# A hybrid transformer layer pair on one core: three gated tile pairs of the input projection moved behind the queries and between the attention's first steps, and gated scaling and memory scaling moved from GpSimd to VectorE and ScalarE

## What is computed

```python
h = rmsnorm(x, norm_mix_g)
proj = h @ w_in                                   # 1024 -> 1988 columns
q, k, v, qi, ki, wi, glu = jnp.split(proj, cuts, axis=-1)
q, k, qi, ki = partial_rope(...)                  # 8 query heads of 64, one key head
a_out = dsa_attention(q, k, v, qi, ki, wi)        # an indexer of 4 heads picks the keys, then softmax
ga, gg = jnp.split(glu, 2, axis=-1)               # 512 + 512 columns
u = causal_dwconv(ga * jax.nn.sigmoid(gg), conv_b_w, conv_b_b)   # 31 taps, 512 channels
b_out = jax.nn.silu(layernorm(u, ln_b_g, ln_b_b))
x = x + jnp.concatenate([a_out, b_out], axis=-1) @ w_out
m = rmsnorm(mem, norm_mem_g)                      # 256 tokens; kc = m @ w_k_cross, vc = m @ w_v_cross
```

## Time and profile before

| | us |
|---|---|
| median of 3 runs | 1429.32 (1425.02 to 1429.35) |
| the profiled execution's own time | 1433.47 |
| its span in the profile | 1431.7 |
| mean granted clock of TensorE | 0.982 of 2.4 GHz |
| busy in the span: TensorE / VectorE / GpSimd / ScalarE | 1369.7 / 789.3 / 606.7 / 539.3 |

### The profile page before, as it was taken

How to read it: one execution, slowest core, us unless ns; L and a number is a source line. 1 busy time by engine, 2 the same in 40 slices (tenths; PEclk the granted TensorE clock), 3 DMA queues, 4 the chain that set the end, 5 groups by cost and what they waited for, 6 DMA issues and landing times.

```text
span 1431.7 us, 18120 instructions
## 1 busy us (share of the span) xinstructions
PE 1369.7 (96%) x6240; PEld 1100.0 (77%) x6240; DVE 789.3 (55%) x1083; ACT 539.3 (38%) x843; POOL 606.7 (42%) x295
## 2 busy tenths in 40 slices
PE   7998888999999999999999999999999999999997
PEld 5787766877678888888888777677778888888885
DVE  6698984253366777777534488555463333333232
ACT  4445667243343232333223353434343223233221
POOL 3587981232144444444444333111234444444341
PEclk9999998999999999999999999999999999999998
DMA  6122320221122232223332222111122322233221
GB/s 218 45 89 88 104 81 23 74 74 66 38 88 89 88 103 91 100 101 106 102 101 82 82 74 75 44 45 45 45 76 100 101 89 103 89 107 101 102 88 73
DMA packets 31874, 121.18 MB, mean 85 GB/s; under 512 B 3536, under 2 KB 3664, under 8 KB 31568
## 3 DMA queue, kind: packets, MB, share of 16 engines
q1 hardware_dynamic: 31392, 119.55, 24.6%
q10 hardware_dynamic: 432, 0.96, 0.3%
HBM read 118.40 MB, written 2.10 MB: 84 GB/s over the span
## 4 chain that ended last, share of the span: by engine, by line
PE 70%; issue 14%; POOL 7%; DVE 5%; ACT 3%; DMA 1%; POOLq 0%; SPq 0%; DVEq 0%; ACTq 0%
PE acc L1627 58%; POOL weights_low L588 4%; PE acc L1775 3%; POOL conv L637 2%; PE aux L1997 1%; PE aux L2017 1%; DVE aux L1160 1%; DVE left L1491 1%; PE aux L1861 1%; PE aux L1999 1%; DMA weights_raw<-w 1%; PE aux L1831 1%; PE aux L1681 0%; PE aux L2033 0%; PE aux L2007 0%
## 5 line engine op out<-in xcount | busy, mean ns | idle before, releaser
L588 POOL TENSOR_TENSOR weights_low<-weights_raw,weights_high 128x1024 fp32r<-128x1024 f32 (+1 forms) x204 | 524.9, 2573 | 794.2 <-ACT weights_high L665 791.2
L665 ACT CAST weights_high<-weights_raw 128x1024 fp32r<-128x1024 f32 (+1 forms) x202 | 222.0, 1099 | 523.3 <-PE acc L1627 502.5
L1627 PE MATMUL acc<-a_high,weights_high 128*128 128x512 f32 x976 | 391.1, 401 | 5.5 <-POOL weights_low L588 3.0
L1627 PE MATMUL acc<-a_high,weights_low 128*128 128x512 f32 x976 | 382.2, 392 | 0.0
L1627 PE MATMUL acc<-a_low,weights_high 128*128 128x512 f32 x976 | 381.8, 391 | 0.0
L1627 PEld LDWEIGHTS acc<-a_high,weights_high 128*128 128x128 f32 x976 | 184.6, 189 | 47.8 <-issue 6.2
L1627 PEld LDWEIGHTS acc<-a_low,weights_high 128*128 128x128 f32 x976 | 184.7, 189 | 39.8 <-issue 2.6
L1627 PEld LDWEIGHTS acc<-a_high,weights_low 128*128 128x128 f32 x976 | 184.3, 189 | 39.2
L1133 DVE TENSOR_TENSOR residual<-acc,residual 128x512 f32<-128x512 f32 (+1 forms) x56 | 38.5, 688 | 183.0 <-PE acc L1627 146.3
L1627 PE MATMUL acc<-h_high,weights_high 128*128 128x512 f32 x352 | 137.6, 391 | 0.0
L1627 PE MATMUL acc<-h_high,weights_low 128*128 128x512 f32 x352 | 137.0, 389 | 0.0
(11 more groups left out here) (346 smaller groups left out, 1898.5 us busy)
## 6 DMA issues: line engine op xcount, KB each, us to landing
weights_raw<-w SPq DMA_DIRECT2D x172, 512.0 KB, 3.2
weights_raw<-w SPq DMA_DIRECT2D x32, 704.0 KB, 4.1
residual<-xT SPq DMA_DIRECT2D x8, 256.0 KB, 7.0
out<-y_tok SPq DMA_DIRECT2D x4, 512.0 KB, 3.6
mem_raw<-memT SPq DMA_DIRECT2D x1, 1024.0 KB, 5.5
mem_tok<-mem SPq DMA_DIRECT2D x1, 1024.0 KB, 7.5
lru_weights<-blockdiag ACTq DMA_DIRECT2D x1, 512.0 KB, 3.4
sine<-positions ACTq DMA_DIRECT2D x1, 256.0 KB, 7.0
```

The costliest lines, as they stand in the source:

```text
L588: g.tensor_tensor(weights_low[:, s, 0:cols], weights_raw[:, s, 0:cols], weights_high[:, s, 0:cols].bitcast(F32), ALU.subtract).then_inc(we ...
L665: a.copy(weights_high[:, s, 0:cols], weights_raw[:, s, 0:cols]).then_inc(weight_high, 1)
L1627: last = t_.matmul(acc[:, bank, 0:cols], w[:, s, wide], x_[:, k0 + k, 0:cols], start=start and k == opens and n == 0, stop=stop and k == c ...
```

## The change

It has four parts.

1. **Chunks and list.** Chunks are ordered `kiwi`, `qiT`, `qiT`, `kv`, the first gated pair (4, 5), the four queries (6 to 9), the other three gated pairs (10 to 15). Tiles 5 and 6 are cut into pieces between the `index` items. The attention's steps begin after tile 9 and the first half of tile 10; eleven half tiles of the gated pairs and the 32 half fills stand between the steps. Twelve of the 16 `best` rounds move into steps 0 to 7, the taps into steps 8 to 27, `mean` from step 25 to 27, and the rest of the layer norm and the out-projection with it by two steps.
2. **Scaling.** VectorE evicts the gated tiles and multiplies by `row_factor` at once (`glu_out`). Memory is scaled in ScalarE's cast, and VectorE makes its low part. GpSimd's items for both are gone.
3. **Head.** TensorE finishes tile 0 before tile 1. ScalarE's squares stand behind all high parts, between which it casts chunks 2 and 3 and copies tiles 0 and 1. `add_x` is interleaved with the angle reduction. The positions are loaded by SyncE's queue behind x. `spread` (the sines) stands behind tile 3.
4. **Convolution.** VectorE has 79 taps (blocks 1, 2 and 17 taps of 3), ScalarE with GpSimd 45.

```diff
-        SHARED_TAPS = 9
-        PRODUCTS = [(1, k) for k in range(SHARED_TAPS)] + [(0, k) for k in range(TAPS)]
-        CONV = [(n, k) for n in (2, 3) for k in range(TAPS)] + [(1, k) for k in range(SHARED_TAPS, TAPS)]
+        SHARED_TAPS = 14
+        PRODUCTS = ([(0, k) for k in range(20)] + [(3, k) for k in range(SHARED_TAPS)]
+                    + [(0, k) for k in range(20, TAPS)])
+        CONV = [(n, k) for n in (1, 2) for k in range(TAPS)] + [(3, k) for k in range(SHARED_TAPS, TAPS)]
...
+        FIRST_PLAN = [("tile", 0, 0, KB), ("tile", 1, 0, KB), ("mem_root",), ("tile", 2, 0, KB),
+                      ("key_turn", 0), ("query_turn", 0), ("tile", 3, 0, 4), ("sum",), ("mem_high", 0, 4),
+                      ("tile", 3, 4, KB), ("mem_low", 0, 4), ("spread",), ("key", 0), ("query", 0),
+                      ("tile", 4, 0, 4), ("query_turn", 1), ("mem_high", 4, 8), ("wi",), ("query", 1),
+                      ("tile", 4, 4, KB)]
...
+        FIRST_PLAN += [("causal",), ("tile", 6, 6, KB), ("gate", 0), ("glu", 0), ("key_turn", 1), ("best",),
+                       ("tile", 7, 0, 4), ("key", 1), ("mem_low", 4, 8), ("query_turn", 2), ("query", 2), ("v",),
+                       ("tile", 7, 4, KB), ("best",), ("tile", 8, 0, 4), ("query_turn", 3), ("query", 3),
+                       ("best",), ("tile", 8, 4, KB), ("mem_spread",), ("tile", 9, 0, 4), ("query_turn", 4),
+                       ("query", 4), ("best",), ("tile", 9, 4, KB)]
+        FILLS = [("tile", n, 4 * half, 4 * half + 4) for n in range(10, 16) for half in range(2)]
+        FILLS += [("fill", n, 4 * half, 4 * half + 4) for n in range(2 * KB) for half in range(2)]
...
-        FILLS_AT = (1, 1, 2, 1, 2, 1, 2, 1, 1, 1, 2, 1, 1, 1, 2, 1, 1, 1, 1, 0, 1, 1, 1, 0, 1, 0, 1, 0, 1, 0, 1, 0)
+        FILLS_AT = (1, 2, 2, 2, 2, 2, 2, 2, 1, 2, 1, 1, 1, 2, 1, 1, 1, 1, 1, 2, 1, 1, 1, 1, 1, 1, 1, 1, 2, 1, 1, 1)
+        BEST_AT = (2, 1, 2, 1, 2, 1, 2, 1)
+        FIRST_TAP, LAST_TAP, FIRST_PRODUCT, LAST_PRODUCT = 8, 27, 0, 25
...
+            if step in (2, 4, 7):
+                FIRST_PLAN += [("gate", (step + 1) // 2 - (step == 7)), ("glu", (step + 1) // 2 - (step == 7))]
...
+            square_x(0)
+            square_x(1)
+            high_next(0, 0)
+            square_x(2)
+            square_x(3)
+            a.copy(kiwi[:], acc[:, 0]).then_inc(tile_out[0], 1)
+            square_x(4)
+            high_next(0, 1)
+            a.copy(qiT[:, 0], acc[:, 1]).then_inc(tile_out[1], 1)
...
-                        act.wait_ge(mem_scaled, k + 1)
-                        a.copy(m_high[:, k], mem_raw[:, k]).then_inc(mem_high, 1)
+                        act.wait_ge(memT_in, 16)
+                        a.activation(m_high[:, k], mem_raw[:, k], ACT.Copy, scale=col("g_mem", k)
+                                     ).then_inc(mem_high, 1)
...
+                        v.scalar_tensor_tensor(m_low[:, k], mem_raw[:, k], col("g_mem", k),
+                                               m_high[:, k].bitcast(F32), ALU.mult, ALU.subtract
+                                               ).then_inc(mem_low, 1)
+                elif what == "glu_out":
+                    b, s = j // 2, j % 2
+                    dve.wait_ge(chunk_done, GLU[j] + 1)
+                    v.tensor_tensor(gate[:, b] if s else glu[:, b, TAPS - 1:TAPS - 1 + T], acc[:, s],
+                                    row_factor[:], ALU.mult).then_inc(tile_out[s], 1)
...
+                for k in range(2, KB):
+                    part(0, k, 0)
+                    part(1, k, 0)
+                    part(0, k, 2)
+                    part(0, k - 2, 1)
+                part(0, KB - 2, 1)
+                part(0, KB - 1, 1).then_inc(chunk_done, 1)
                 for k in range(KB):
+                    part(1, k, 1)
+                for k in range(KB):
+                    last = part(1, k, 2)
+                last.then_inc(chunk_done, 1)
```

192 lines of the change are left out of this document (84 added, 108 removed).

## The result

| | median us | lowest to highest | runs |
|---|---|---|---|
| before, beside it | 1428.95 | 1425.02 to 1430.89 | 7 |
| after | 1437.47 | 1433.17 to 1442.6 | 7 |

The ratio is 1.006, 95% interval 1.0045 to 1.0075: the change costs 8.5 us, and I had forecast 1.3. The profiled execution of after took 1433.41 us, as long as that of before (1433.47), so the two traces have to be compared place by place and not at their ends.

The account below looks back on a forecast made before the run. TensorE, busy 96% of the span, leaves only idle and slow stretches to win; VectorE is fullest after 130 us. Head +7.4, VectorE's run -3.0, tail -2.6 give +1.8; 1429.3 plus that less 0.5 is 1430.6 us, range 1419 to 1437.

Parts of the forecast that it names:

- Head: Start to the last index score's causal mask: sines behind tile 3 delay VectorE, so the end comes 7.4 us later.
- the index wait: TensorE before the first index product: a new wait of about 4.2 us for VectorE, with a slow clock behind it.
- VectorE's run: Causal mask to the mean's start: 143.5 us of work plus 10 idle, 153.5 instead of 156.5, a gain of 3.0 us.
- Tail: Mean to out-projection: more half fills in the last steps leave less work behind the wait, a gain of 2.6 us.
- The same 9 us chain: Tail, from the factor's spread to the end of TensorE's wait: unchanged at 9 us, from +20.3 to +29.3 after the mean.
- the stall itself: Tail, TensorE's wait for ScalarE behind the spread: claimed to stay near 5 us.
- The stall at 192.75: TensorE's 2.74 us stall, where vc's copy now has wider steps beside it: should shrink, 0.5 us gained.
- GpSimd's relief at nothing: Attention: taking gated and memory scalings off GpSimd was valued at zero, since VectorE's listed waits had no GpSimd in them.
- B: Rival: VectorE idles 4 us instead of 10 and the tail's half-clock stretch doesn't come; 1421.7 us, chance 0.33.
- C: Rival, steps 0 to 7: gated tiles wait for VectorE's evictions, engines in lockstep, +6.3 us; 1436.9 us, chance 0.17.
- D: Rival, steps 0 to 7: ScalarE's three pairs of table loads aren't hidden, 7.7 us; 1438.3 us, chance 0.07.
- the wait behind the spread: Sign in the tail that the forecast is right: TensorE waits 5 us for ScalarE behind the factor's spread.

Follow-up runs that it names:

- e12: The changed kernel with sines early, memory's work later, sines times the factors in PSUM, and three fills moved to steps 11, 14 and 21; 1426.74 us.
- e14: e12 with four pieces of one tile between the index scores instead of six of two, tile 6 whole behind the causal mask; 1428.32 us.
- e18: e14 with one selection round of VectorE moved from step 0 to in front of the second key's rope; 1428.89 us.
- e17: e13 with three taps moved from VectorE to products of ScalarE and GpSimd (12 shared taps instead of 9); 1420.29 us.
- e6: The changed kernel with gated tiles again copied by ScalarE and scaled on GpSimd, all else as changed; 1437.81 us.
- e16: e12 with three taps moved from VectorE to products of ScalarE and GpSimd (17 shared taps instead of 14); 1431.15 us.
- e13: e9 with the eight gated tiles evicted and scaled by VectorE instead of ScalarE's copy and GpSimd's scaling; 1420.41 us.
- e15: e12 with the three moved fills put back, five again in steps 28 to 31; 1431.44 us.
- e5: The changed kernel with both sines right behind the root of the sums and memory's work behind the first keys and queries; 1437.33 us.
- e9: e8 with VectorE multiplying the sines by the rows' factors in PSUM and copying the factors to SBUF afterwards; 1419.60 us.
- e1: The changed kernel with the sines moved to right behind the norm's root; 1441.55 us.
- e3: The kernel before with the change's new head alone, the sines right behind the norm's root; 1423.45 us.
- e8: e3 with GpSimd's eight memory scalings in pairs behind every third index score; 1424.31 us.

## Why the prediction was wrong

- **Head, +7.4 forecast, +5.4 measured.** Right in kind. Tile 2 began at 20.6 (23.6 forecast), the sine product at 39.9 (42.4), the index wait was 4.18 us (4.2) with the half-clock pieces behind it, the mask at 66.9 (68.9). The 2 us come from tiles 0 and 1, which ended 3 us sooner than I had reckoned. What I had not seen is that this shift isn't all lost time: 3.3 us of it are tile 6's pieces done ahead (e12 against e14).
- **VectorE's run, -3.0 forecast, -1.5 measured** (155.0 us for 156.5). Its work was 143.5 us to the tenth; its idle time 11.5 instead of 10. TensorE had 44.2 us of work in steps 0 to 7, not 40.3, as much as VectorE there. The mean at 221.9 lies in the forecast 221 to 223. The sum was near, but not the picture of one bound engine: a shorter or earlier list of VectorE gained at most 0.7 us at the mean (e18), nothing in e17, and the mean came later where GpSimd got the work (e6, e16); adding work to it in the old order cost nothing (e13).
- **Tail, -2.6 forecast, +4.5 measured** (34.4 us became 38.9). This is the step that failed, by 7.1 us, as much as the whole error of 7.2 (8.5 for 1.3); the errors of head and run, -2.0 and +1.5, nearly cancel, which is luck. "The same 9 us chain ends at +29.3": the chain was neither the same nor in time. It starts where the factor's spread ends (TensorE, before and then after):

```profile
236.38 1.11 PE L1681 MATMUL aux<-ident,small 128*128 128x128 f32 x8
```

```profile
244.38 1.11 PE L1695 MATMUL aux<-ident,small 128*128 128x128 f32 x8
```

  Counted from the mean that is +19.5 and +23.6, where I had +20.3 for after: the sum for the mean took 5.40 us instead of 3.70, a half fill more (1.5 us) stands ahead of the variance, and the next one, behind the variance, ran mostly at half clock (0.63 us a piece). From there to the end of the wait it took 11.15 us and not 9: "the stall itself stays, near 5 us" left out that the last fill's cast and two evictions, 2.1 us, now stand on ScalarE between the silus and the copy TensorE waits for; it waited 7.18 us. Behind the wait came 4.2 us and not 3.0, again at half clock. These are 3.3, 2.1 and 1.2 us, and before's own tail was 0.5 shorter than I had reckoned. e15 against e12 prices the three fills in these steps at 4.8 us. I had booked them as cover for the wait; they were a load on the chain that makes the wait. The half clock of the mean's sum isn't explained: it stood behind a wait of 1.85 us, but in e5 and e6 the sum took 3.70 us behind waits of 1.83 and 1.86, and e5's tail was as long as after's (38.86), with more pieces at half clock later on.
- **The stall at 192.75, -0.5:** it stayed, 2.8 us at 210.07.
- **GpSimd's relief at nothing:** right for the old order (e13: no gain); in the changed one it is worth 2.4 us at the mean (e6), after VectorE's added evictions are paid.
- **Rivals.** B fell: the idle time did not go. C fell: TensorE's waits for evictions in steps 0 to 7 are 0.3 us. D fell: no wait behind a table load, and no drain behind any of the six. The result, slower by over 0.3%, had 0.24, all of it put on C and D; no rival on the slow side had the tail as its place. The signs named beforehand didn't tell the two apart either: the index wait and the mean came as forecast, the sines 2.5 us and tile 2 3 us sooner, and only the wait behind the spread, 7.2 us for 5, pointed at the tail.

What of the change is good is its new head: with the sines early and their factors in PSUM, in the old order, it makes the kernel 9 us faster than before (e9). Queries ahead of the gated pairs, with what goes with them, cost 7 us against that (e12 against e9, first tile 250.5 for 243.3). Of the parts in which these two differ, the gated scaling is cleared (e13); memory's scaling and low parts, the split of the taps and the late mean have no run of their own. That VectorE's taps start 14 us later is shown; which loop then sets the 77 us behind it stays open between VectorE's list, 73.1 us, and the round of ScalarE's products, GpSimd's additions and low parts, 70.5 us on GpSimd. e16 shows that the time doesn't follow VectorE's list alone, and it grew by as much as GpSimd's work did; but the opposite trial, fewer products and more taps, wasn't made, and e16 was also granted a lower clock (0.96 behind step 8).

## What to carry to other kernels

Work put into a late stage to cover a wait has its own casts and evictions, and they queue on the engine that the wait is for: count them there before booking the cover. When two engines are both over 90% busy in a stretch, a shorter list on one may be worth nothing until the other's is shorter too (e16, e18); ask then when the longest list can start. And if VectorE and GpSimd work side by side, keep one operand of VectorE's urgent operations in PSUM, or let them begin before GpSimd does.

## What the runs showed of the hardware

The two products of sines and factors (VectorE, 128x512, both operands in SBUF) took 2.87 to 2.94 us if they began beside a low part of GpSimd (2.4 us), in four runs (e1, e3, e5, e8), and 0.68 to 0.69 otherwise. Other operations of VectorE were held too: two additions of squares in after's head took 2.79 and 2.69 us, and the masks of the chosen keys, which read one tensor in SBUF and write to SBUF, 0.90 us for three in before, 2.5 in after and 4.8 in e6. With an operand in PSUM a product of that size took 0.70 us beside a low part (e9).

One short wait less can be worth more than itself: at the first index score, at 1.60 us of idle TensorE's pieces went on at 0.40 us, and at 3.84 and 4.18 they took 0.63. The length of one wait isn't enough to tell: behind 2.81 us the pieces took 0.63 in before (28.59) and 0.40 in after (210.07). And code that is the same took 1179.3 us in one execution and 1170.8 in another, with the granted clock 0.91 and 1.00 in one of its stretches: a profiled total can hide the whole effect of a change.
